# Attention by pairs of heads with stationary values, normalised ahead of the turn; weight tiles released ahead of evictions

## What is computed

```python
def causal_block_attention(q, k, v, scale):
    for blk in range(S // Q_BLOCK):                     # Q_BLOCK = 128, S = 1024
        q0 = blk * Q_BLOCK
        kend = q0 + Q_BLOCK
        qb = q[:, q0:kend]
        s = jnp.einsum('bqhd,bkhd->bhqk', qb, k[:, :kend]).astype(jnp.float32) * scale
        mask = jnp.arange(kend)[None, :] <= (q0 + jnp.arange(Q_BLOCK))[:, None]
        s = jnp.where(mask, s, jnp.float32(-1e30))
        prob = jax.nn.softmax(s, axis=-1).astype(v.dtype)
        outs.append(jnp.einsum('bhqk,bkhd->bqhd', prob, v[:, :kend]))
```

## Time and profile before

| what | us |
|---|---|
| median of 3 runs | 4064.01 |
| lowest and highest | 4061.86, 4067.34 |
| the profiled execution | 4065.56 |
| its span, first to last instruction | 4064.3 |

### The profile page before, as it was taken

How to read it: one execution, slowest core, us unless ns; L and a number is a source line. 1 busy time by engine, 2 the same in 40 slices (tenths; PEclk the granted TensorE clock), 3 DMA queues, 4 the chain that set the end, 5 groups by cost and what they waited for, 6 DMA issues and landing times.

```text
span 4064.3 us, 44734 instructions
## 1 busy us (share of the span) xinstructions
PE 3753.2 (92%) x18398; PEld 3094.9 (76%) x18398; DVE 1815.3 (45%) x2380; ACT 1317.5 (32%) x2129; POOL 1172.0 (29%) x624
## 2 busy tenths in 40 slices
PE   5998998979799987999999898999987989999998
PEld 4786877878777766888888767777666868888886
DVE  3435444444155534233233353887543444444435
ACT  3323132222344323221221343776123233232323
POOL 3322313231100232333333211576133313222321
PEclk8988898988999999999999999999999999999999
DMA  4101010000100343111111222222344421111111
GB/s 119 53 1 53 1 46 19 19 29 18 39 12 1 99 144 95 50 50 47 50 49 47 73 88 86 70 86 86 99 154 143 148 80 50 47 48 51 47 47 52
DMA packets 282074, 253.63 MB, mean 62 GB/s; under 512 B 11333, under 2 KB 221569, under 8 KB 281872
## 3 DMA queue, kind: packets, MB, share of 16 engines
q1 hardware_dynamic: 267264, 216.52, 17.7%
q10 hardware_dynamic: 11520, 25.17, 1.6%
q0 software_dynamic: 3088, 9.10, 0.6%
HBM read 214.04 MB, written 36.70 MB: 62 GB/s over the span
## 4 chain that ended last, share of the span: by engine, by line


## 5 line engine op out<-in xcount | busy, mean ns | idle before, releaser
L401 POOL TENSOR_TENSOR weight_lo<-stage,weight_hi 128x1024 fp32r<-128x1024 f32 (+4 forms) x265 | 634.5, 2400 | 1551.9 <-ACT weight_hi L393 1551.7
L364 PE MATMUL psum<-hT_hi,weight_hi 128*128 128x512 f32 x2240 | 895.8, 400 | 13.7 <-ACT sig_g L744 6.6
L365 PE MATMUL psum<-hT_lo,weight_hi 128*128 128x512 f32 x2240 | 882.0, 394 | 0.0
L366 PE MATMUL psum<-hT_hi,weight_lo 128*128 128x512 f32 x2240 | 881.3, 393 | 0.0
L364 PEld LDWEIGHTS psum<-hT_hi,weight_hi 128*128 128x128 f32 x2240 | 427.9, 191 | 112.3 <-issue 16.0
L365 PEld LDWEIGHTS psum<-hT_lo,weight_hi 128*128 128x128 f32 x2240 | 427.2, 191 | 93.8 <-issue 6.1
L366 PEld LDWEIGHTS psum<-hT_hi,weight_lo 128*128 128x128 f32 x2240 | 426.3, 190 | 89.8
L393 ACT ACTIVATE weight_hi<-stage 128x1024 fp32r<-128x1024 f32 (+4 forms) x329 | 313.5, 974 | 462.2 <-PE psum L366 381.7
L1935 DVE TENSOR_TENSOR x<-x,psum 128x512 f32<-128x512 f32 x432 | 290.1, 686 | 216.4 <-PE psum L366 215.8
L364 PE MATMUL psum<-weight_hi,act_hi 128*128 128x512 f32 x864 | 339.9, 393 | 0.0
L366 PE MATMUL psum<-weight_hi,act_lo 128*128 128x512 f32 x864 | 339.4, 393 | 0.0
(11 more groups left out here) (371 smaller groups left out, 6045.9 us busy)
## 6 DMA issues: line engine op xcount, KB each, us to landing
stage<-in_w_in SPq DMA_DIRECT2D x64, 512.0 KB, 4.0
stage<-in_w_up SPq DMA_DIRECT2D x44, 512.0 KB, 3.9
scratch_gates<-gate ACTq DMA_DIRECT2D x64, 256.0 KB, 2.0
gs<-scratch_gates SPq DMA_DIRECT2D x64, 256.0 KB, 2.8
stage<-in_w_out SPq DMA_DIRECT2D x32, 512.0 KB, 4.8
stage<-in_w_ffn_up SPq DMA_DIRECT2D x32, 512.0 KB, 4.0
stage<-in_w_ffn_down SPq DMA_DIRECT2D x32, 512.0 KB, 3.9
stage<-in_w_down SPq DMA_DIRECT2D x22, 512.0 KB, 3.4
```

The lines of the kernel that those rows point to most:

```text
L364: q.matmul(out, stat[0], mov[0], start=first, stop=False)
L365: q.matmul(out, stat[0], mov[1], start=False, stop=False)
L366: return q.matmul(out, stat[1], mov[0], start=False, stop=final)
L401: g.q.tensor_tensor(lo, K.staged(w), hi.bitcast(F32), ALU.subtract).then_inc(*S.w_lo_pool.up(w))
```

## The change

Three parts.

**Attention.** A unit is now a pair and a query block, with both heads, 32 units. Head h has its own score banks 2h, or 2h and 2h+1. P is scaled on VectorE by the reciprocal of its row sum after the exponent (`dve_exponent`) and before the turn. The output product has the values as the stationary operand, 64 columns for each head in its half of the columns, and moves 128 columns of the turned P; the heads alternate. The product comes out turned, with both heads above each other on 128 partitions, so that ScalarE copies it straight to the high part and VectorE makes the low part; `otok` and `pair_out` are gone. The turned P goes round banks 4 to 6, in four buffers instead of three. The loop takes score(i), turn(i-1), output(i-2), exponent(i), and two feed steps at each place.

**RWKV chunks.** A gram step is a chunk with both heads: B products of head 0 and 1, then K products of head 0 and 1. VectorE's step has both masks.

**Release.** In the compression, the merge and the down products, `released` comes behind the last tile's product but ahead of its evictions, which have steps of their own (`compressed`, `merge_rows`, `down_rows`).

```diff
-        elif ring == "work":
-            banks = (3 + self.ring_at["work"] % 4,)
-            self.ring_at["work"] += 1
+        elif ring == "turned":
+            banks = (4 + self.ring_at["turned"] % 3,)
+            self.ring_at["turned"] += 1
...
+def pe_gram(K, blk, n, side, i):
+    pe, c = K.pe, 2 * n + i
+    b = [K.open(("gram", blk, n, 2 * i + h)) for h in range(2)]
     pe.wait_ge(K.S.act_evac, ("tok", blk, 3, 4))
-    rhs = K.AR[hd(h), c, :, :]
-    pe.q.matmul(b[:, 0:2 * P], K.Bt[hd(h), c, :], rhs, start=True, stop=True)
-    pe.q.matmul(b[:, 2 * P:4 * P], K.Kt[hd(h), c, :], rhs, start=True, stop=True).then_inc(*K.S.mm.up(("gram", blk, n, q)))
...
+    for o, left in ((0, K.Bt), (2 * P, K.Kt)):
+        for h in range(2):
+            mm = pe.q.matmul(b[h][:, o:o + 2 * P], left[hd(h), c, :], K.AR[hd(h), c, :, :], start=True, stop=True)
+            if o:
+                mm.then_inc(*K.S.mm.up(("gram", blk, n, 2 * i + h)))
...
-TURN_LAG, OUT_LAG = 2, 1
-UNITS = [(pair, h, qb) for pair in range(HEADS // 2) for h in range(2) for qb in QB_ORDER]
+TURN_LAG, OUT_LAG = 1, 1
+UNITS = [(pair, qb) for pair in range(HEADS // 2) for qb in QB_ORDER]
...
-def unit_banks(u):
-    return (2,) if UNITS[u][2] < 4 else (0, 1)
+def score_banks(u, h):
+    return (2 * h,) if UNITS[u][1] < 4 else (2 * h, 2 * h + 1)
...
+def dve_exponent(K, u):
+
+    v, S, (pair, qb) = K.v, K.S, UNITS[u]
+    n = (qb + 1) * P
+    for h in range(2):
+        c, rows = 2 * u + h, unit_rows(K, u, h)[0]
+        v.wait_ge(S.act_evac, ("exp", u, h))
+        v.step(v.q.reciprocal(K.st[:, 3, c:c + 1], K.st[:, 2, c:c + 1]))
+        v.q.tensor_scalar(rows[:, 0:n], rows[:, 0:n], K.st[:, 3, c:c + 1], None, ALU.mult).then_inc(*S.dve_op.up(("P", u, h)))
...
+            b = K.open(("PT", u, h, j0), "turned")
+            pe.wait_ge(S.dve_op, ("P", u, h))
...
     for j in range(qb + 1):
-        mm = pe.q.matmul(b[:, 0:VDIM], K.PT[u % len(K.PT)][:, j, :], K.vh[pair % 2][:, j, h, :], start=j == 0, stop=j == qb)
+        for h in range(2):
+            mm = pe.q.matmul(b[hd(h), 0:P], K.vh[pair % 2][:, j, h, :], unit_rows(K, u, h)[1][:, j, :], start=j == 0, stop=j == qb)
     mm.then_inc(*S.mm.up(("o", u)))
...
+def act_output(K, u):
+    a, S, (pair, qb) = K.a, K.S, UNITS[u]
+    a.wait_ge(S.mm, ("o", u))
+    a.q.activation(K.oT[0][:, pair, qb * P:(qb + 1) * P], K.bank(("o", u))[:, 0:P], ACT.Copy).then_inc(*S.br_hi.up(("oT", u)))
...
     v, S, (pair, qb) = K.v, K.S, UNITS[u]
+    hi, lo = (o[:, pair, qb * P:(qb + 1) * P] for o in K.oT)
+    v.wait_ge(S.br_hi, ("oT", u))
+    v.q.tensor_tensor(lo, K.bank(("o", u))[:, 0:P], hi.bitcast(F32), ALU.subtract).then_inc(*S.br_lo_dve.up(("oT", u)))
+    K.free(("o", u), S.br_lo_dve)
...
@@ order_compressed
             o.do("compress", part, t, w0)
-        o.released(tiles)
+            if t == NT - 1:
+                o.released(tiles)
+            o.do("compressed", part, t)
@@ order_attention
-                fed = -3
+                fed = -2
             o.do("score", i)
         fed += 1
-        more = 1 if fed > 0 else 0
+        more = 2 if fed > 0 else 0
         advance(feed, more)
         if 0 <= i - TURN_LAG < len(UNITS):
             o.do("turn_p", i - TURN_LAG)
         advance(feed, more)
...
+        if i - TURN_LAG - OUT_LAG >= 0:
+            o.do("output", i - TURN_LAG - OUT_LAG)
         advance(feed, more)
         if i < len(UNITS):
             o.do("exponent", i)
@@ order_merge
-                o.do("merge_out", m, part, t, n, w0, pre[t])
+                o.do("merge_out", m, part, t, n, w0)
                 if t == tokens - 1:
                     o.released(4)
+                o.do("merge_rows", m, part, t, n, pre[t])
@@ order_ffn
                     o.do("down", f, i, t, n, w)
-                o.released()
+                    if t == NT - 1:
+                        o.released()
+                    o.do("down_rows", f, i, t, n)
```

More of the change, by code:

```diff
@@ L283, in restart @@
             q.seen, q.latest = {}, None
-        self.ring_at = {"all": 0, "work": 0}
+        self.ring_at = {"all": 0, "turned": 0}
         self.holder = {}
@@ L1485, in dve_head_turn @@
     if pair >= 2:
-        v.wait_ge(S.mm, ("o", 16 * (pair - 1) - 1))
+        v.wait_ge(S.mm, ("score", NT * (pair - 1) - 1, 1))
     dst = (K.qT if name == "q" else K.kT)[pair % 2]
@@ L1490, in dve_head_turn, with unit_rows @@
     K.free(key, S.dve_evac)
-def unit_banks(u):
-    return (2,) if UNITS[u][2] < 4 else (0, 1)
+def score_banks(u, h):
+    return (2 * h,) if UNITS[u][1] < 4 else (2 * h, 2 * h + 1)
+def unit_rows(K, u, h):
+    return K.Pm[2 * (u % 2) + h], K.PT[2 * (u % 2) + h]
 def pe_score(K, u):
-    pe, S, (pair, h, qb) = K.pe, K.S, UNITS[u]
+    pe, S, (pair, qb) = K.pe, K.S, UNITS[u]
     n = (qb + 1) * P
[L1500 to L1506, removed]
+    for h in range(2):
+        sc = K.open(("score", u, h), score_banks(u, h))
+        pe.wait_ge(S.dve_evac, ("heads", pair))
+        for k0 in range(0, n, HALF):
+            w = min(HALF, n - k0)
+            mm = pe.q.matmul(sc[:, k0:k0 + w], K.qT[pair % 2][0:QK, h, qb * P:(qb + 1) * P], K.kT[pair % 2][0:QK, h, k0:k0 + w],
+                             start=True, stop=True)
+        mm.then_inc(*S.mm.up(("score", u, h)))
@@ L1541, in pt_part @@
-def pt_part(K, u, j0):
-    qb = UNITS[u][2]
-    nj = min(4, qb + 1 - j0)
-    return K.PT[u % len(K.PT)][:, j0:j0 + nj, :], K.bank(("PT", u, j0))[:, 0:nj * P].rearrange("p (j c) -> p j c", j=nj)
+    for h in range(2):
+        c = 2 * u + h
+        a.wait_ge(S.dve_op, ("max", u, h))
+        if u >= 2:
+            a.wait_ge(S.mm, ("PT", u - 2, h))
+        a.q.activation(unit_rows(K, u, h)[0][:, 0:n], K.bank(("score", u, h))[:, 0:n], ACT.Exp, bias=K.st[:, 1, c:c + 1],
+                       scale=SCALE, accum_out=K.st[:, 2, c:c + 1]).then_inc(*S.act_evac.up(("exp", u, h)))
+        K.free(("score", u, h), S.act_evac)
@@ L1589, in dve_output @@
-    K.free(("o", u), S.dve_evac)
-def pe_pair_out(K, pair, t0):
-    b = K.open(("oT", pair, t0), "work")
-    K.pe.wait_ge(K.S.dve_evac, ("o", 16 * pair + 15))
-    for i in range(4):
-        mm = K.pe.q.transpose(b[:, i * P:(i + 1) * P], K.otok[:, t0 + i, :], K.ident[:, :])
-    mm.then_inc(*K.S.mm.up(("oT", pair, t0)))
-def act_pair_out(K, pair, t0):
-    a, S = K.a, K.S
-    a.wait_ge(S.mm, ("oT", pair, t0))
-    a.q.activation(K.oT[0][:, pair, t0 * P:(t0 + 4) * P], K.bank(("oT", pair, t0)), ACT.Copy).then_inc(*S.br_hi.up(("oT", pair, t0)))
@@ L1754, in sp_residual, with pe_merge_out @@
     K.res_after[m][slot] = (m, tt, n)
-def pe_merge_out(K, m, part, t, n, w0, slot):
+def pe_merge_out(K, m, part, t, n, w0):
     pe, S = K.pe, K.S
@@ L1774, in pe_merge_out, with dve_merge_rows @@
             mm.then_inc(*S.mm.up(("tile", w)))
-def dve_merge_out(K, m, part, t, n, w0, slot):
+def dve_merge_rows(K, m, part, t, n, slot):
     v, S, spec = K.v, K.S, spec_of(K, m)
@@ L2425, in lay_out @@
     K.vh = [put("vh", [P, NT, 2, VDIM]) for _ in range(2)]
[L2426 to L2427 removed]
+    K.qtok, K.ktok = put("qtok", [P, NT, 2, QK]), put("ktok", [P, NT, 2, QK])
+    K.Pm, K.PT = [put("P", [P, S]) for _ in range(4)], [put("PT", [P, NT, P]) for _ in range(4)]
     K.st = put("st", [P, 4, HEADS * NT])
@@ L2707, in order_batch @@
 def order_batch(o, blk, n, side):
-    for q in range(4):
-        o.do("gram", blk, n, side, q)
+    for i in range(2):
+        o.do("gram", blk, n, side, i)
         yield
```

150 lines of the change are left out of this document (63 added, 87 removed).

## The result

The changed kernel takes **4038.33 us** (median of 4 runs, 4032.83 to 4040.34), against 4065.58 for the kernel before beside it (4 runs, 4061.86 to 4067.34). The ratio is 0.9932, with a 95% interval of 0.9915 to 0.9949: faster by 27 us, where 23 to 25 were forecast.

The account below looks back on a forecast made before the run. TensorE was taken as the bound, busy in 92% of the span. Terms -7 - 3.6 - 25.4 + 11.5 = -24.5 from the profiled 4065.56 gave 4041 us; the forecast holds from 4028 to 4054, full range 4018 to 4074.

Parts of the forecast that it names:

- chunk products: Recurrence: first side's masks complete one mask earlier, 0.6 us in four phases, 1.2 in four slow ones; -7 us.
- compression: Earlier release lets weight splits, transfer and norm move up: -2.9 and -0.75 us, together -3.6, at worst 0.
- merges: Both merges: splits start ahead of the last token tile's evictions, shortening TensorE's idle times; -25.4 us, bounds -8 to -30.
- attention: Four pairs of heads: less TensorE work but new waits and lower-level time; +11.5 us, range 0 to +25.
- the change of form: Attention: shape change around each output group, 0.14 us per pair of changes, 4.5 in all; 7.0 by the skill's rule.
- the lower clock: Attention: about five stretches with TensorE at its lower level, 8 us, against 6.3 us before.
- the walk through the queues: Attention, middle pair: scores wait 9.4 us for exponents behind output copies, 3.2 for rotated queries; four pairs 247.5.
- The 2.7 for the ring of three banks: Attention, middle pair: turns wait 2.7 us for a bank that VectorE has not yet copied out.
- rival A: Attention stays bound by TensorE's work, exponents end in time: attention -37 us, time 3993; chance 0.06.
- B: Attention: column halves don't run side by side, records keep a 0.112 us slot: 4074.5 us, slower by 10; chance 0.06.
- C: Merges: the earlier splits don't pay, -8 us instead of -25.4, time 4058; chance 0.12.
- D: Attention: gaps hold TensorE at the lower level for half of the stage, +35 us instead of +11.5, time 4065; chance 0.10.

Follow-up runs that it names:

- e2: The kernel before with the chunk products alone in the new order: 4052.59 us, ratio 0.9961.
- e3: The kernel before with the earlier releases alone (compression, merges, down products): 4035.49 us, ratio 0.9924.
- e10: The earlier release in the merges alone, on the kernel before; compression and down products as before: 4038.49 us, ratio 0.9936.
- e1: The kernel before with the attention part alone: 4086.45 us, ratio 1.0052.
- e4: The changed kernel with the exponents of unit i moved ahead of the output of unit i-2: 4005.90 us, ratio to before 0.9854.
- e5: The kernel of e4 with the rotation of the next pair's queries ahead of its key/value projections: 3991.15 us, ratio to before 0.9812.
- e7: The changed kernel with a unit's output products all of head 0, then all of head 1: 4063.02 us, ratio to before 0.9988.
- e9: The kernel of e2 with TensorE's products in the old sequence, B and K of head 0, then of head 1: 4049.02 us, ratio 0.9965.

## Why the prediction was right, and where its terms were off

The total of 4041 was met within 3 us, but by terms of which two were off in opposite directions: the chunk products gave 6 to 9 us more than their term, and the attention cost 5 to 9 more than its own. That these cancel is luck.

| term | predicted | in the trace after | alone |
|---|---|---|---|
| chunk products | -7 | -15.8, by the end of the first stage | -13 (e2) |
| compression | -3.6 | -3.0 | -3 to -5 (e3 less e10) |
| merges | -25.4 | -15.5 and -12.0 | -25 (e10) |
| attention | +11.5 | +16.5 | +21 (e1) |

**Attention: the mechanism was right, two terms were too small.** The slot of the output records is the 0.055 that was taken: 32 of them take 1.90 us to the next product (1191.85 to 1193.75) and 4 take 0.37 (1204.36 to 1204.73), so 28 more take 1.53. What is left of either group is 0.15 us, whatever its length. Ahead of a group the change of form shows once more: eight turns before one take 0.97 us (1315.48 to 1316.45), where eight turns take 0.87, so 0.10. Together that is 0.25 us a group where the prediction took 0.14: it had read 0.11 on the way in and 0.05 in the first group, and put the way back at nothing. The trace has 31 groups (the last two units stand together): 31 x 0.11 is 3.4 us. The Trainium skill, TensorEngine Tiling (Array Packing), Key Properties, says that a change of tiling mode drains TensorE. The trace agrees for both directions, and its 31 x 0.25 = 7.8 us stand nearer to the 7.0 that the prediction worked out by that rule than to the 4.5 that it used.

The other term is the lower clock. At a share of 0.96 over 260.7 us the stage loses 10.4 us against full clock, where the step had 8; the last pair, at 0.94, loses 3.3 of them. These 3.4 and 2.4 cover the missing 5 us (260.7 for 255.5). The forecast of 65.5, 68.5, 68.5 and 52 came out as 65.9, 68.7, 71.6 and 54.6; the first two are met, and the last two carry the slow stretches.

The waits came where the walk through the queues put them, each score behind an exponent behind an output copy, as e4 shows by taking them away. In the second pair the scores' 9.4 shows as 7.7 and the rotation's 3.2 as 2.9. The 2.7 for the ring of three banks shows as 0.8 at most, all that the turns of P wait there. Idle time is counted from a record's modelled end, which lies behind the next possible start, so it comes out short, and the walk's sum of waits can't be checked term by term.

What the prediction did not ask is whether those waits belong to the change of form at all. For the greater part they don't: they come from the place of one step in a list. The prediction priced an order of queues and took it for the price of two-head units. So rival A, with the stage at 207 us, looked remote, while one moved step took the stage from 260.7 to 228.6 and a second one to 216.0.

**Chunk products: half of the gain was missed.** VectorE's order gave the 0.6, as worked out. The changed kernel, VectorE's masks and GpSimd's first level:

```profile
176.48 4.87 DVE L947 TENSOR_TENSOR m<-psum,mask 128x512 f32<-128x512 f32 x8 [0.83 <-PE psum L936]
```

```profile
180.33 2.48 POOL L963 TENSOR_TENSOR Al<-m,levels 128x512 f32<-128x512 f32 x2 [9.26 <-DVE m L947]
```

From the first mask to the first level it is 3.85 us (180.33 - 176.48); before it was 4.71 (182.49 - 177.78). One mask is 0.61 of it. The other 0.25 is time that VectorE spent, before, between its first mask (177.78) and the seven of the earlier trace rows (178.65), waiting for products; now its eight masks stand in one row, since the products come closer: 8 records in 0.87 us where they took 0.98. The bigger miss is in the four phases with a low clock at the start. TensorE in the changed kernel:

```profile
236.93 1.23 PE L936 MATMUL psum<-AR,Bt 64*128 64x256 f32 x4
237.94 1.06 PE L936 MATMUL psum<-AR,Kt 64*128 64x256 f32 x4
...
241.90 0.59 PE L936 MATMUL psum<-AR,Kt 64*128 64x256 f32 x4
```

TensorE and VectorE before, in the same phase:

```profile
240.93 1.22 PE L935 MATMUL psum<-AR,Bt 64*128 64x256 f32 x4
...
242.81 1.22 PE L935 MATMUL psum<-AR,Bt 64*128 64x256 f32 x4
```

```profile
242.88 1.29 DVE L944 TENSOR_TENSOR m<-psum,mask 128x512 f32<-128x512 f32 x2 [1.01 <-PE psum L936]
```

From 236.93 to the last group the products take 4.97 us, from 239.06 before it was 7.73. There VectorE waits for TensorE, so the products set the phase, not one mask of VectorE; I had doubled the 0.6 instead of asking what ends last at the lower clock. Two things shortened them. At the lower clock eight records took 1.88 us before (240.93 to 242.81) and take 1.70 now (238.80 to 240.50, in the rows left out), 0.7 for the 32 of a phase. And the clock rose earlier in this phase: its share went from 0.59 over 8.8 us to 0.70 over 6.4, which is 7.2 us at the lower level before and 3.8 now. In e2 the four gave -1.9 each instead of -1.2. In the changed kernel the eight phases hold 11.3 of the stage's 15.8 us. Another 1.3 lie ahead of the first phase (176.65 to 175.34), where nothing was changed, and the rest is not placed.

**Compression and merges: right in kind, place and size.** The last norm of the first merge and its like in the second wait 4.92 and 5.08 us, where the earlier trace rows had 8.86 and 9.33, so -3.9 and -4.3 for the predicted -3.85 and -4.2:

```profile
1587.27 0.90 PE L530 MATMUL psum<-ident,xn 128*128 128x128 f32 x3 [4.92 <-DVE xn L519]
```

```profile
3284.34 0.69 PE L530 MATMUL psum<-ident,xn 128*128 128x128 f32 x2 [5.08 <-DVE xn L519]
```

ScalarE at the end of the first merge. The splits come ahead of the last square, the fourth waits 3.79 for its transfer (4.55), and the square, which has the norm behind it, follows 1.9 us after that split ends:

```profile
1572.93 1.06 ACT L393 ACTIVATE weight_hi<-stage 128x1024 fp32r<-128x1024 f32 x1
...
1580.50 1.06 ACT L393 ACTIVATE weight_hi<-stage 128x1024 fp32r<-128x1024 f32 x1 [3.79 <-DMA stage<-in_w_ffn_down]
1583.46 0.60 ACT L1798 ACTIVATE psum<-x 128x512 f32<-128x512 f32 x1 [1.89 <-DVE x L1787]
```

The idle times of 4.12, 2.83 and 2.85 us are gone. The slow stretch of the earlier trace rows went with them: 27 records at full clock where 18 took as long.

```profile
1550.70:1557.80 7.10, 5.03 (x27) 1.00 0.89 235
```

The compression has 11.67 for 14.75, -3.1 for the -2.9, and its fourth split still waits, 3.31 us:

```profile
1045.83 0.24 PE L1337 MATMUL psum<-ident,posr 8*128 8x8 f32 x1 [11.67 <-DVE posr L1344]
```

```profile
1037.16 0.63 ACT L393 ACTIVATE weight_hi<-stage 128x512 fp32r<-128x512 f32 x1 [3.31 <-DMA stage<-in_w_o_rwkv]
```

**Rivals.** B (halves don't overlap) needed a spacing above 0.108; it is 0.055, and e7, where most of the overlap is lost, shows what that costs, +25. C fell with e3, D with the clock shares. A is what e4 and e5 make of the kernel, in good part.

## What to carry to other kernels

When work is taken off the busiest engine and the stage grows, look for the step that frees what the engine fills next and see what stands ahead of it in its own queue: one evacuation that waits for the busiest engine's latest product, put ahead of one whose input has long been there, cost 32 us here, and moving it was a change of two lines. A side chain whose inputs are complete (the rotation) belongs in the list where they are complete. At a lower clock ask again which engine ends last: a term is not simply doubled. And a change of form on the busiest engine is priced on the way in and on the way back.

## What the runs showed of the hardware

fp32 products with 64 stationary and 128 moving columns, in opposite column halves and in turn, took 0.055 us a record, half of the 0.109 of full-width turns of as many columns. Each group of them cost 0.25 us besides, 0.10 ahead of it and 0.15 within and behind it. With the halves no longer in turn (e7), groups with two or four records of a half in a row took the same time (0.37 and 0.60 for 0.37 and 0.59), and a group with 16 in a row took 3.26 for 1.90.

In the row halves, records of 256 columns stood 0.122 us apart with four products of a half in a row (before), 0.109 with two (e9) and 0.108 in turn (e2). Full-width records of 256 columns took 0.216 (eight from 1210.39 to 1212.12 in the changed kernel), so the halves ran side by side in all three orders, and alternating them gained little.

More idle time of TensorE went along with a lower clock, but did not fix it. In attention TensorE was idle for 14.4 us in e5, 18.7 before, 24.0 in e4, 47.5 in e7, 48.9 in e1 and 49.3 in the changed kernel, with clock shares of 0.98, 0.98, 0.97, 0.94, 0.94 and 0.96.
